# Hybrid pooling and retention encoder layer on 8 cores: pooled half of the output projection first in the last four chunks, the last chunk in halves, pooled groups and q alternating in the last block

## The reference

```python
mod = silu(c) @ ada_w + ada_b                      # shift, scale, gate
h = rms_norm(x, g_pre) * (1 + scale) + shift
u_pool, q, k, v, z = split(h @ w_in)               # 1024, 1024, 1024, 1024, 2048
# pool: 4 groups, windows 2, 4, 8, 16: centred mean minus token, per-group linear, channel scale
# retention: 8 heads of 128, rotary q and k, forward and backward scans over chunks of 128
#            (two decays), sum of both, then per-head group norm
y = concat(y_pool, y_ret) * silu(z)                # 2048 wide
out = y @ w_out                                    # 2048 x 1024
return x + gate * rms_norm(out, g_post)
```

## Time and profile before

| | |
|---|---|
| median of 3 runs | 3080.69 us (3077.94 to 3084.44) |
| profiled execution | 3075.19 us |
| span of its slowest core (core 4) | 3073.6 us |
| spans of the eight cores | 3057.6 to 3073.6 us |
| TensorE busy | 2958.0 us, 96% |
| VectorE busy | 2017.3 us, 66% |
| GpSimd busy | 1537.7 us, 50% |
| ScalarE busy | 1048.2 us, 34% |

### The profile page before, as it was taken

How to read it: one execution, slowest core, us unless ns; L and a number is a source line. 1 busy time by engine, 2 the same in 40 slices (tenths; PEclk the granted TensorE clock), 3 DMA queues, 4 the chain that set the end, 5 groups by cost and what they waited for, 6 DMA issues and landing times.

```text
span 3073.6 us, 51814 instructions; the slowest of 8 cores (3057.6 to 3073.6 us)
## 1 busy us (share of the span) xinstructions
PE 2958.0 (96%) x16981; PEld 1498.9 (49%) x17306; DVE 2017.3 (66%) x1956; ACT 1048.2 (34%) x1265; POOL 1537.7 (50%) x1374
## 2 busy tenths in 40 slices
PE   4799999999999999999999999999999999999997
PEld 3444444444444444444455555555555555555554
DVE  3556888888787787787655555555555555555554
ACT  4343444443333333332233333333333333323332
POOL 4565555655555566555444444444444444444442
PEclk9878999999999999999999999999999999999999
DMA  9757885565565568564667788777778787788783
GB/s 194 194 147 187 196 216 169 160 205 173 163 193 168 160 193 218 164 194 145 192 177 198 189 208 186 205 190 196 195 200 201 196 196 202 195 201 197 196 188 111
DMA packets 631224, 573.28 MB, mean 187 GB/s; under 512 B 416634, under 2 KB 491434, under 8 KB 624816
## 3 DMA queue, kind: packets, MB, share of 16 engines
q1 hardware_dynamic: 614688, 539.55, 65.0%
q0 software_dynamic: 16272, 30.41, 5.9%
HBM read 284.34 MB, written 208.15 MB: 160 GB/s over the span
## 4 chain that ended last, share of the span: by engine, by line
PE 87%; DVE 4%; issue 3%; DMA 3%; POOL 2%; ACT 1%; SPq 0%; another core or an unknown queue 0%; DVEq 0%; POOLq 0%; ACTq 0%
PE psum L604 27%; PE psum L1430 21%; PE psum L1341 11%; PE psum L1301 11%; PE psum L700 9%; PE psum L1380 4%; PE psum L767 3%; DMA t_adaw<-ada_w 1%; PE psum L1361 1%; PE psum L647 1%; DMA t_xin<-x 1%; DVE t_t L620 1%; POOL t_S L731 1%; DVE psum L621 0%; DVE t_qA L622 0%
## 5 line engine op out<-in xcount | busy, mean ns | idle before, releaser
L604 PE MATMUL psum<-t_wv,t_hT 128*128 128x512 bf16 x1505 | 359.3, 390 | 18.1 <-DVE t_qA L622 7.9
L1430 PE MATMUL psum<-t_wout,t_ypB 128*128 128x512 bf16 x1531 | 363.4, 380 | 3.1 <-DVE t_yT L1413 1.0
L1430 PE MATMUL psum<-t_wout,t_yT 128*128 128x512 bf16 x1448 | 358.7, 379 | 4.8 <-issue 0.2
L700 PE MATMUL psum<-t_hT,t_wu 128*128 128x512 bf16 x1496 | 355.1, 386 | 3.8 <-ACT t_wu L1013 1.6
L604 PE MATMUL psum<-t_wq,t_hT 128*128 128x512 bf16 x1511 | 349.3, 383 | 9.8 <-DMA t_wq<-w_in 4.5
L1341 PE MATMUL psum<-t_wz,t_hB 128*128 128x512 bf16 x1532 | 346.6, 379 | 0.7 <-DVE t_yb L1400 0.5
L1354 POOL TENSOR_TENSOR t_kf<-t_krB,t_kdf 128x1024 bf16<-128x1024 bf16 x94 | 226.7, 2411 | 222.8 <-PE psum L767 214.8
L1400 DVE TENSOR_TENSOR t_yb<-psum,t_szr 128x1024 bf16<-128x1024 f32 x96 | 117.5, 1224 | 330.7 <-POOL t_szr L1398 330.7
L1301 PE MATMUL psum<-t_hB,t_wz 128*128 128x512 bf16 x1443 | 327.9, 379 | 5.7 <-ACT t_sz L1345 0.4
L604 PE MATMUL psum<-t_wk,t_hT 128*128 128x512 bf16 x1369 | 318.3, 382 | 3.7 <-DVE t_hT L593 1.2
L620 DVE TENSOR_TENSOR t_t<-psum,t_rt 128x1024 f32<-128x1024 f32 x176 | 214.4, 1218 | 138.8 <-PE psum L604 137.8
(11 more groups left out here) (181 smaller groups left out, 4764.5 us busy)
## 6 DMA issues: line engine op xcount, KB each, us to landing
t_xr<-x SPq DMA_DIRECT2D x96, 512.0 KB, 5.3
y<-t_xr SPq DMA_DIRECT2D x96, 512.0 KB, 4.9
t_xin<-x SPq DMA_DIRECT2D x88, 512.0 KB, 5.9
hscr<-t_hT SPq DMA_DIRECT2D x24, 1024.0 KB, 5.7
vscr<-t_vA SPq DMA_DIRECT2D x96, 256.0 KB, 4.6
t_vB<-vscr SPq DMA_DIRECT2D x96, 256.0 KB, 4.9
t_hB<-hscr SPq DMA_DIRECT2D x24, 1024.0 KB, 7.1
t_ypB<-pscr SPq DMA_DIRECT2D x24, 1024.0 KB, 6.5
```

Of the source, the lines that this page charges most:

```text
L604: last = e.matmul(pp.f(half * 512, half * 512 + 512), hTt[:, dc, j * 128:(j + 1) * 128], w_sb[:, dc, half * 512:half * 512 + 512], start=( ...
L700: r = e.matmul(pu.f(i * 512, i * 512 + 512), wu_sb[:, dc, (2 * g + i) * 128:(2 * g + i + 1) * 128], hTt[:, dc, :], start=(dc == 0), stop=( ...
L1430: last = e.matmul(pout.f(half * 512, half * 512 + 512), l_, wout_sb[:, ec, half * 512:(half + 1) * 512], start=(ec == 0), stop=(ec == 15))
```

## The change

Four edits:

- In the last block of the first phase, one pooled group and one q alternate; k, v and the state follow as before.
- `outB` of the last four chunks (92 to 95) issues its matmuls in two parts: first the eight pooled ones of both column halves, which no longer wait for `t_yT`, then the eight retention ones of both halves.
- In chunk 95 the group norm (square, sum, three GpSimd operations, product, transposes, copy) runs in two halves of four heads, with the transposes in the banks of `stp`. The end of chunk 95 runs in two halves of 512 columns, with a DMA of 256 KB for each.
- In every chunk the end is ordered anew: VectorE multiplies the PSUM result by the gate table at once (the product no longer needs the norm), and then one operation multiplies by the norm and adds x. The factor sqrt(1024) moves into the gate table (`gate`).

```diff
-            for g in range(4):
-                doU(seq, b, slot, g)
-            for j in js:
+            for ji, j in enumerate(js):
+                doU(seq, b, slot, ji)
                 sl = nxt_sl(seq, b * BLK + j)
                 rtload(b * BLK + j, sl)
                 doQ(seq, b * BLK + j, slot, j, sl)
...
+        nh = 2 if g == ng - 1 else 1
+        hw_ = 8 // nh
+        py = stp
...
+        for i in range(nh):
+            h0, h1 = i * hw_, (i + 1) * hw_
+            a0, a1 = h0 * 128, h1 * 128
+            pb = po.b if nh == 1 else [po.b[i]]
+            act(lambda e, a0=a0, a1=a1: e.activation(out=o2t[:, a0:a1], in_=po.f(a0, a1), func=AF.Square), r=pb + ([o2b] if i else []), w=[o2bs[i]])
...
+        split = 2 if g >= ng - BLK else 1
+        for part in range(split):
+            for half in range(2):
+                def outmm(e, half=half, part=part):
+                    r_ = None
+                    for e8 in range(part * 8, 16 if split == 1 else part * 8 + 8):
...
+                pe(outmm, r=([] if part else ypb) + ([] if split == 2 and part == 0 else [yTb]) + wout_b, w=[pout.b[half]])
+        halves = 2 if g == ng - 1 else 1
...
+            act(lambda e, i=i, a0=a0, a1=a1: e.activation(out=junk[:, a0:a1], in_=pout.f(a0, a1), func=AF.Square,
+                                                          accum_out=st_t[:, 24 + i:25 + i]), r=pb, w=[stb, junk_b])
+            if i == 0:
+                prod(0)
+        if halves == 2:
+            dve(lambda e: e.scalar_tensor_tensor(out=st_t[:, 26:27], in0=st_t[:, 24:25], scalar=float(D) * EPS, in1=st_t[:, 25:26],
+                                                 op0=ALU.add, op1=ALU.add), r=[stb], w=[stb])
...
+        if halves == 2:
+            prod(1)
+        for i in range(halves):
...
+            dve(lambda e, a0=a0, a1=a1: e.scalar_tensor_tensor(out=xrt[:, a0:a1], in0=outs_t[:, a0:a1], scalar=st_t[:, 27:28],
+                                                               in1=xrt[:, a0:a1], op0=ALU.mult, op1=ALU.add),
+                r=[outsb, stb] + ([xrb] if i else []), w=[xb_])
```

More of the change, by code:

```diff
@@ L1407, in try_ @@
                 last = None
-                pv = py.bf(0).rearrange("p (dc t) -> p dc t", dc=8)
-                for h in range(8):
+                pv = py.bf(i).rearrange("p (dc t) -> p dc t", dc=8)
+                for h in range(h0, h1):
                     last = e.transpose(pv[:, h, :], ybt[:, h, :], ident[:, :])
                 return last
-            pe(try_, r=[ybb, ident_b], w=[py.b[0]])
-            dve(lambda e: e.tensor_copy(out=fl(yT[k][0]), in_=py.bf(0)), r=[py.b[0]], w=[yT[k][1]])
+            pe(try_, r=[ybbs[i], ident_b], w=[py.b[i]])
@@ L1415, in outB @@
+            dve(lambda e, a0=a0, a1=a1, i=i: e.tensor_copy(out=fl(yT[k][0])[:, a0:a1], in_=py.bf(i)[:, a0:a1]), r=[py.b[i]], w=[yT[k][1]])
+    xr2b = Buf("xr2")
+    o2x, stx, szrx, ybx = (Buf(n) for n in ("o2x", "stx", "szrx", "ybx"))
     def outB(g):
@@ L1424, in outB @@
         pout = Pair()
-        for half in range(2):
-            def outmm(e, half=half):
-                last = None
-                for ec in range(16):
-                    l_ = ypt[:, ec, j * 128:(j + 1) * 128] if ec < 8 else yTt[:, ec - 8, :]
-                    last = e.matmul(pout.f(half * 512, half * 512 + 512), l_, wout_sb[:, ec, half * 512:(half + 1) * 512],
-                                    start=(ec == 0), stop=(ec == 15))
-                return last
-            pe(outmm, r=ypb + [yTb] + wout_b, w=[pout.b[half]])
@@ L1439, in outB @@
-        dve(lambda e: e.tensor_tensor(out=xrt[:, :], in0=xrt[:, :], in1=outs_t[:, :], op=ALU.add), r=[xrb, outsb], w=[xrb])
-        sch.dma("sp", ys[s].ap()[c * 128:(c + 1) * 128, :], xrt[:, :], r=[xrb], w=[drb("y", s, c)], key=xrb)
+        split = 2 if g >= ng - BLK else 1
[4 more added lines that the diff above has]
+                    for e8 in range(part * 8, 16 if split == 1 else part * 8 + 8):
+                        l_ = yTt[:, e8 - 8, :] if e8 >= 8 else ypt[:, e8, j * 128:(j + 1) * 128]
+                        r_ = e.matmul(pout.f(half * 512, half * 512 + 512), l_, wout_sb[:, e8, half * 512:(half + 1) * 512],
+                                      start=(e8 == 0), stop=(e8 == 15))
+                    return r_
+                pe(outmm, r=([] if part else ypb) + ([] if split == 2 and part == 0 else [yTb]) + wout_b, w=[pout.b[half]])
@@ new lines, in outB @@
+        if halves == 2:
+            prod(1)
+        for i in range(halves):
+            a0, a1 = i * wd, (i + 1) * wd
+            xb_, yb_ = (xrb, drb("y", s, c)) if i == 0 else (xr2b, drb("y2", s, c))
+            dve(lambda e, a0=a0, a1=a1: e.scalar_tensor_tensor(out=xrt[:, a0:a1], in0=outs_t[:, a0:a1], scalar=st_t[:, 27:28],
+                                                               in1=xrt[:, a0:a1], op0=ALU.mult, op1=ALU.add),
+                r=[outsb, stb] + ([xrb] if i else []), w=[xb_])
+            sch.dma("sp", ys[s].ap()[c * 128:(c + 1) * 128, a0:a1], xrt[:, a0:a1], r=[xb_], w=[yb_], key=xb_)
```

35 lines of the change are left out of this document (29 added, 6 removed).

## The result

The changed kernel takes **3095.36 us** (median of 13 runs) against 3082.28 us for the kernel before (median of 13 runs). The ratio is 1.0048, with a 95% interval from 1.0028 to 1.0069, so it is slower by half a per cent. The forecast was 3067.8, within 3062 to 3077, so it is wrong in size and in sign. The time is also above the third rival's 3076.7, and what happened resembles the fourth rival, which had 0.09.

A forecast was written before the change was run, and what follows sets the result against it. TensorE was taken to bound the ordinary chunks, leaving only its idle or slow time to gain. Terms -4.0 - 5.1 - 1.5 - 0.1 - 2.2 = -12.9 us gave a median of 3067.8 us, range 3062 to 3077.

The forecast's parts named there:

- third rival: Simulated queues do not come out as the edit reads; only about -4 us is left, 3076.7; chance 0.12.
- fourth rival: Earlier pout release rewrites ordinary chunks' queues; a 0.46 us wait for t_yb in each gives +42, 3110; chance 0.09.
- Part 5: New end in every chunk: VectorE frees pout about 1 us sooner, but TensorE is full already, so 0 us.
- signs that I had named for a wrong forecast: Second-phase stretch below 198 busy; t_yT half 1 wait with clock below 1.00; new t_qA or t_kbA wait between 1490 and 1510.
- Part 1: Last block of the first phase: alternating pooled groups and q removes TensorE stops, -4.0 us, bounds 0 and -4.5.
- waits that I feared: First phase's last block: new TensorE waits for t_qA or t_kbA between 1490 and 1510; t_kbA late by at most 3 us.
- Parts 2 to 4: Tail, chunks 92 to 95: pooled matmuls first, group norm and end in halves, -8.9 us together.
- Part 3: Before chunk 95's retention output: eight pooled matmuls of chunk 94 fill the 1.58 us mask wait, -1.5; ring waits -0.1.
- bound of +2: Upper bound in the tail: a pair held by an early pooled part keeps scores or po waiting.
- second rival: Chunk 95's group norm comes late, TensorE waits and runs its last 16 matmuls slow; sum -8.9, 3071.8; chance 0.10.
- part 2: Chunk 95 after its retention output: 16 pooled projection matmuls fill the group norm's gap, no slow clock, -5.1 us.
- Part 4: End of chunk 95 in halves: 5.16 to 3.6 us (-1.6), last DMA -0.6 (bounds 0 and -0.9), together -2.2.

The follow-up runs named there:

- e5: Instructions of the kernel before, the simulation told that the old end's addition is 0.6 us shorter: ratio 1.0151, undisturbed cores 3092.7 us (+33.0).
- e8: Changed kernel with the call of zT recorded after the chunk's retention instead of at the loop's end: undisturbed cores 3048.6 us (-11.1 against before), no ratio.
- e7: Changed kernel, same instructions, the simulation told that the mask is ready 0.5 us later: ratio 0.9971, undisturbed cores 3050.2 us (-9.5 against before).
- e1: Changed kernel with the old end in all chunks but the last: 3072.21 us, ratio 0.996, undisturbed cores 3049.5 us (-10.2 against before).
- e4: Kernel before with only the tail edits (pooled matmuls first in the last four chunks, chunk 95 in halves): undisturbed cores 3054.7 us (-5.0), no ratio.
- e6: Changed kernel, same instructions, the simulation told that the product is ready 1.0 us later: ratio 0.9976, undisturbed cores 3048.2 us (-11.5 against before).
- e10: e1 with pooled matmuls first in chunk 95 alone: 3053.63 us in one execution, beside 3068.75 for the kernel before.
- e9: e1 with no pooled matmuls first in any chunk: 3054.64 us in one execution, beside 3068.75 for the kernel before.

## Why the prediction was wrong

**Part 5 failed**: "TensorE is full already, so I take 0." It is full as long as its queue is the same, and the queue is a result of the edit. Measured it is +19.9 us over the ordinary chunks, 0.22 us per chunk. The steps, as e5 to e8 bear them out:
1. The product no longer waits for GpSimd's norm, so in the simulation VectorE is done with the old chunk's end sooner.
2. The mask behind it is then bound by the scores and not by VectorE. This is visible in both traces, and e7 shows that it decides: 0.5 us on this one operation gives the old order.
3. With the mask sooner, `o` is ready after half a call of `zT`, and the greedy order puts it there. The other half lands behind the projection. (That `o` displaces the half is read from the two orders; no run took the simulation apart further.)
4. The pair is held for 13 us, and the gate waits until `t_yb`, at the end of ScalarE, VectorE and GpSimd's group norm, has given back the pair of `o`. The projection and the eight matmuls are not quite long enough to hide this, by 0.3 us in most chunks (16.35 - 16.05). The simulation did not see this: in the times that it gives the written program of after, `t_yb` ends 8.1 us behind the retention output, less than the 8.6 of these 40 matmuls; in the trace it is 8.9 (2213.88 + 0.22 to 2221.81 + 1.21).

**The fourth rival** had the right place (queues of the ordinary chunks, a wait for `t_yb` once in each) and was wrong in two points. It took the 0.46 of the earlier trace rows for each chunk, +42; the waits were about 0.3 and came in seven chunks of ten (61 of 87). And it named as trigger the earlier release of `pout`. Told of an earlier release alone, the simulation keeps before's order, and told of a release 0.5 to 1.0 us later alone it keeps after's; this was read from the written queues and not run. What I put against the rival, that the simulated costs of the two operations are unchanged, was no argument: an order is made of costs and of what each operation waits for, and the second was what the edit changed. The profile of before had the sign. The mask was never late for the scores; it started at 2208.50, when VectorE's addition ended, 1.2 us after the scores. A queue on the path was timed by an engine that is 57% busy. And of the signs that I had named for a wrong forecast one came true: a stretch of after is busy for 197.20 of 200. (The 198.68 of before was itself too low by missing records; core 0 of the same execution has 200.00.)

**Part 1 is right.** On core 2 the eight matmuls of the state ahead of this block start at 1440.01 before and at 1439.35 after, and the first L1301 of the second phase at 1503.83 and 1499.26: 63.82 us and 59.91, -3.9, forecast -4.0. (The other 0.7 of the -4.6 in the table lie ahead of the edited block.) On all eight cores of after it is 59.9; before has 63.8 on five and 64.6 to 64.8 on three. The waits for `t_U` are gone, pooled groups and q follow each other without a gap, and one of the waits that I feared is there:

```profile
1448.43 3.62 PE L700 MATMUL psum<-t_hT,t_wu 128*128 128x512 bf16 x16
1451.88 3.62 PE L604 MATMUL psum<-t_wq,t_hT 128*128 128x512 bf16 x16
...
1482.39 0.61 PE L767 MATMUL psum<-t_vA,t_kbA 128*128 128x128 bf16 x8 [0.99 <-POOL t_kbA L784]
```

**Parts 2 to 4 are too large together, and two of their terms had the wrong mechanism** (the room before the retention output, and the last DMA): -8.9 forecast, -6.1 in e1 and e4, and -4.2 in after, whose chunks 93 to 95 are ordered differently again. From the start of chunk 95's retention output on TensorE to the end of the last matmul it is 20.45 us on core 2 of before (3033.58 to 3054.03) and 13.66 on core 1 of e1 (3026.03 to 3039.69), forecast 13.8. So what is missing lies outside this stretch: some 0.6 behind it, and 2.3 ahead of it. From the scores of chunk 95 to its retention output it is 2.19 us on core 2 of before (3031.39 to 3033.58) and 4.51 on core 1 of e1 (3021.52 to 3026.03), and the other cores of both agree within 0.02; from the Square of 92 to these scores nothing changed (33.08 and 33.04). TensorE, core 1 of e1:

```profile
3022.57 3.61 PE L1448 MATMUL psum<-t_wout,t_ypB 128*128 128x512 bf16 x16 [0.44 <-DVE t_outs L1458]
3026.92 3.62 PE L1448 MATMUL psum<-t_wout,t_yT 128*128 128x512 bf16 x16
3030.37 1.89 PE L1448 MATMUL psum<-t_wout,t_ypB 128*128 128x512 bf16 x8
3032.10 0.38 PE L1423 MATMUL psum<-t_ident,t_yb 128*128 128x128 bf16 x4
3032.32 1.89 PE L1448 MATMUL psum<-t_wout,t_ypB 128*128 128x512 bf16 x8
3034.18 0.38 PE L1423 MATMUL psum<-t_ident,t_yb 128*128 128x128 bf16 x4
3036.08 3.61 PE L1448 MATMUL psum<-t_wout,t_yT 128*128 128x512 bf16 x16 [1.52 <-DVE t_yT L1426]
```

**Part 3 is the term that failed here**, forecast -1.6, with a bound of +2. I gave the wait of 1.58 eight pooled matmuls of chunk 94; sixteen went there (3022.57), after a wait of 0.44 for a pair, and held the retention output up until 3026.03, though the mask was ready at 3023.57 + 1.22 = 3024.79. The mask itself started 2.05 us after the start of the scores instead of 0.71, because VectorE did the end of chunk 93 first (L1460 at 3022.43). The held pair that I had given as a bound is real, but it is only the 0.44 of this.

That the stretch behind it came out at 13.66 is partly luck, two misses that cancel. It holds eight matmuls fewer than I had counted (1.73 us), and they are missing as cover: TensorE ran out of work 1.52 us before the last 16. The copy it waited for was late in part by VectorE's queue, core 1 of e1:

```profile
3032.95 0.42 DVE L1426 COPY t_yT<-psum 128x512 bf16<-128x512 bf16 x1 [0.99 <-PE psum L1423]
3033.34 0.69 DVE L1413 TENSOR_TENSOR t_yb<-psum,t_szr 128x512 bf16<-128x512 f32 x1
3034.33 1.28 DVE L1458 SCALAR_TENSOR_TENSOR t_outs<-psum,t_st,t_ggtab 128x1024 f32<-128x1024 f32 x1 [0.29 <-POOL t_st L1457]
3035.53 0.41 DVE L1426 COPY t_yT<-psum 128x512 bf16<-128x512 bf16 x1
```

Chunk 94's end (L1458) stands ahead of the second copy. The first copy found VectorE free and started 0.47 after its transposes (3032.10 + 0.38 = 3032.48); the second, with transposes until 3034.18 + 0.38 = 3034.56, starts at 3035.53, 0.97 after them, so some 0.5 of the 1.52 are VectorE's queue. The group norm in halves itself ran as forecast: half 1 is through GpSimd 7.2 us after the start of the retention output, forecast 7.1.

**The second rival's** late group norm came in part (the wait of 1.52), and its slow last matmuls did not. The granted clock stayed 1.00 (2.4 GHz) around this wait in e1, core 1, and the stretch takes 13.7 us on all eight cores:

```profile
3028.00:3034.00 6.00, 6.00 (x32) 2.69 (x30) 2.60 (x5) 1.19 (x3) 5.07 (x8) 1.00 0.20 79
3034.00:3040.00 6.00, 4.18 (x21) 1.73 (x20) 3.48 (x5) 0.84 (x3) 0.15 (x1) 1.00 0.21 87
```

Before it averaged 0.66 after the waits of 1.99 and 1.05. But not on every core, so idling alone does not decide it. On core 3 of before it stayed 1.00 in the stretch that follows the same waits:

```profile
3042.00:3047.00 5.00, 4.18 (x20) 1.97 (x21) 2.98 (x3) 0.00 (x0) 0.00 (x0) 1.00 0.20 80
```

From the start of the retention output to the last matmul it is 18.8 us on cores 3, 6 and 7 of before, and 20.3 to 20.5 (four cores) or 21.6 (one) on the others. So on three cores the 1.9 us of slow matmuls in part 2's 5.1 were not there to be gained.

**Part 4**: from the last matmul's end to VectorE's last result it is 5.17 us on core 2 of before, and 3.58 to 3.60 on all eight cores of after, forecast 3.6. VectorE, core 2 of after:

```profile
3065.99 0.69 DVE L1456 TENSOR_TENSOR t_outs<-psum,t_ggtab 128x512 f32<-128x512 f32 x1 [1.90 <-ACT t_junk L1461]
3067.60 0.16 DVE L1466 SCALAR_TENSOR_TENSOR t_st<-t_st 128x1 f32<-128x1 f32 x1 [0.92 <-ACT t_junk L1461]
3067.70 0.69 DVE L1456 TENSOR_TENSOR t_outs<-psum,t_ggtab 128x512 f32<-128x512 f32 x1
3068.64 1.61 DVE L1476 SCALAR_TENSOR_TENSOR t_xr<-t_outs,t_st,t_xr 128x512 f32<-128x512 f32 x2 [0.24 <-POOL t_st L1470]
```

But the 0.6 of the last DMA didn't come. From VectorE's last result to the end of the span it is 3.8 us on the eight cores of before and 3.8 on those of after. This is my bound 0, and the reason I gave for it, a fixed cost of the DMA, is wrong too: the transfer is not on the path. SP (SyncE) on core 2 of before and then of after, behind the last DMA's issue (count; shortest, median and longest duration in ns; first and last start):

```profile
L358 SPq EVENT_SEMAPHORE  x62: 17/17/17, 3059.7 to 3062.7; - x62
L358 SPq EVENT_SEMAPHORE  x63: 17/17/17, 3070.7 to 3073.8; - x63
```

These are the waits that `finish` writes for the semaphore of every DMA buffer. SP issues the last DMA at 3059.33 and passes them one by one, 0.05 us apart, until 3062.75; the span ends 0.27 later. The 512 KB had landed 2.6 us after their issue, some 3061.9, and no wait of the row is longer than the others. After, the last 256 KB are issued at 3070.32 and land about 2.1 us later, and the row lasts until 3073.79. It takes 3.04 us on all eight cores of before and 3.09 on those of after, with one semaphore more. No run shortened it, so what lies behind it is not shown. The Trainium skill, "DMA: Bandwidth & Descriptors", section on the anatomy of one DMA, fits a part by size beside its fixed cost on another issuing path, an estimated 0.6 us for the 256 KB saved; the two landings, 2.6 and 2.1 us, are near that, and the end of this program can't show it.

**The versions.** e1 is faster than before by 0.40% (0.26 to 0.54%), and 23.3 us faster than after by its undisturbed cores. e6, e7 and e8 keep the new end with another order and lie within 1.3 us of e1's undisturbed cores, which these runs can't tell apart. e10 had the shortest spans, a median of 3046.6 over its eight cores against 3060.8 for before in the same comparison, in one execution each.

## What to carry to other kernels

Where a simulation writes the queues, no edit is local: read the new order of the bounding engine before adding up terms, and do it again for edits on engines that have time to spare. In the profile, look for operations that feed the bounding engine and start when their own engine comes free, rather than when their input does; an edit that frees that engine moves them, and with them the order. A product in two halves that share a pair of banks should close before anything long, since a half-filled pair is one pair less for all that stands between. In a tail that is filled with early work, look at what each piece holds up: one chunk of it was better here than four, and with either, sixteen matmuls in a gap that had room for eight delayed the retention output behind them. And before a last transfer is made shorter, look at what its queue does behind it: here a row of waits outlasted it.

## What the hardware showed that I had not expected

SyncE passes a row of waits that are already fulfilled at 0.05 us each: 62 of them take 3.04 us at the end of before, on all eight cores, and outlast a DMA of 512 KB that lands 2.6 us after its issue. And the granted clock is not decided by the gaps alone: after the same waits of 2.0 and 1.05 us it fell on five cores of before (0.66 over the next 5 us on core 2) and stayed 1.00 on three; e9, with waits of 1.13 and 0.78, also has both kinds of core (60.4 and 62.1 us); and a gap of 1.52 us cost nothing on any core of e1 (1.00 in 3034 to 3040 on core 1).
